# Routing numbers made between the output projection's slabs, and the sums of two norms with operands exchanged

## The reference

```python
x = first_block(...)            # ends: return rms_norm(h, norm_final)[:, N_META:]
mod = (c @ w_ada[l] + b_ada[l])[:, None, :]
shift1, scale1, gate1, shift2, scale2, gate2 = jnp.split(mod, 6, axis=-1)
h = rmsnorm(x, norm1_w[l]) * (1.0 + scale1) + shift1
proj = h @ w_in[l]
...
x = x + gate1 * (merged @ w_out[l])
h2 = rmsnorm(x, norm2_w[l]) * (1.0 + scale2) + shift2
x = x + gate2 * hierarchical_moe(h2, w_rg, b_rg, w_re, b_re, w_gate, w_up, w_down)

def hierarchical_moe(h, ...):
    g_logits = hf @ w_rg + b_rg                 # 4 groups
    pg = jax.nn.softmax(g_logits, axis=-1)
    pg_top, g_idx = lax.top_k(pg, 1)
    e_logits = hf @ w_re + b_re                 # 32 experts; those of the best group are looked at
    pe_top, j_idx = lax.top_k(softmax(e_sel), 2)
    weights = pg_top * pe_top / sum(pe_top)
    y = sum over the two experts of weight * (silu(hf @ w_gate[e]) * (hf @ w_up[e])) @ w_down[e]
```

## Time and profile before

| | |
|---|---|
| Median of 3 runs | 1809.47 us (1806.29 to 1811.33) |
| The profiled execution | 1804.85 us, its span 1803.0 us |
| PE busy | 1649.4 us, 91% of the span |
| DVE, ACT, POOL busy | 803.3, 541.7, 54.4 us |
| Mean granted clock of PE | 0.956 of full speed |
| HBM traffic | 268 MB, 149 GB/s over the span |

### The profile page before, as it was taken

The page is one execution under the profiler, slowest core; times in us unless marked ns, Lnnn a source line. Parts: engine busy times, 40 slices in busy tenths (PEclk is TensorE's granted clock), DMA queues, the critical chain, the costliest instruction groups (busy, mean ns, idle before and its releaser), DMA issues.

```text
span 1803.0 us, 20227 instructions
## 1 busy us (share of the span) xinstructions
PE 1649.4 (91%) x8343; PEld 1229.9 (68%) x8343; DVE 803.3 (45%) x1325; ACT 541.7 (30%) x851; POOL 54.4 (3%) x75
## 2 busy tenths in 40 slices
PE   3999999999997899999999999999999987987782
PEld 3996777777786688888888686797678855432330
DVE  5455334444452666665222864436653543110113
ACT  5234344354432322222112423322353312110111
POOL 3000000000000000000000000000000000111100
PEclk8999999999998899999998999999999987999997
DMA  4332212222232446473222222212123724999994
GB/s 130 106 94 70 71 48 71 71 71 71 67 98 94 140 157 219 162 233 130 104 94 65 70 71 71 70 48 71 48 71 140 264 113 162 417 419 421 419 381 161
DMA packets 146256, 260.33 MB, mean 144 GB/s; under 512 B 16036, under 2 KB 120640, under 8 KB 132464
## 3 DMA queue, kind: packets, MB, share of 16 engines
q1 hardware_dynamic: 140240, 249.82, 39.3%
q0 software_dynamic: 5920, 9.16, 1.4%
HBM read 253.71 MB, written 14.68 MB: 149 GB/s over the span
## 4 chain that ended last, share of the span: by engine, by line
PE 84%; DVE 7%; issue 4%; ACT 2%; DMA 2%; SPq 0%; POOLq 0%; DVEq 0%; ACTq 0%
PE psum L2220 20%; PE psum L2221 19%; PE psum L2222 19%; PE psum L2783 7%; PE psum L2800 3%; PE psum L2529 1%; PE psum L2518 1%; PE psum L2501 1%; PE psum L2761 1%; PE psum L2302 1%; DVE WL L1420 1%; PE psum L2410 1%; PE psum L2614 1%; PE psum L2713 1%; ACT Sb L1012 1%
## 5 line engine op out<-in xcount | busy, mean ns | idle before, releaser
L2220 PE MATMUL psum<-AH,WH 128*128 128x512 f32 (+1 forms) x1240 | 492.6, 397 | 16.5 <-DVE AL L1466 6.0
L2221 PE MATMUL psum<-AL,WH 128*128 128x512 f32 (+1 forms) x1240 | 476.3, 384 | 0.0
L2222 PE MATMUL psum<-AH,WL 128*128 128x512 f32 (+1 forms) x1240 | 473.0, 381 | 0.0
L1420 DVE TENSOR_TENSOR WL<-raw,WH 128x2048 fp32r<-128x2048 f32 (+1 forms) x100 | 226.6, 2267 | 207.8 <-ACT WH L916 207.3
L2220 PEld LDWEIGHTS psum<-AH,WH 128*128 128x128 f32 x1240 | 236.6, 191 | 81.5 <-issue 20.1
L2222 PEld LDWEIGHTS psum<-AH,WL 128*128 128x128 f32 x1240 | 237.0, 191 | 46.9
L2221 PEld LDWEIGHTS psum<-AL,WH 128*128 128x128 f32 x1240 | 237.0, 191 | 44.4 <-issue 3.1
L916 ACT ACTIVATE WH<-raw 128x2048 fp32r<-128x2048 f32 (+1 forms) x100 | 189.0, 1890 | 148.8 <-PE psum L2222 109.9
L2783 PE MATMUL psum<-WE,XT 128*64 128x512 f32 x544 | 131.0, 636 | 28.6 <-issue 27.7
L2783 PEld LDWEIGHTS psum<-WE,XT 128*64 128x64 f32 x544 | 47.4, 147 | 110.5 <-issue 110.5
L1833 DVE SCALAR_TENSOR_TENSOR cst<-araw,pcol,cst 128x256 f32<-128x256 f32 x168 | 81.6, 485 | 6.0
(11 more groups left out here) (483 smaller groups left out, 1891.4 us busy)
## 6 DMA issues: line engine op xcount, KB each, us to landing
raw<-w_in SPq DMA_DIRECT2D x45, 1024.0 KB, 5.2
WE<-w_gate SPq DMA_DIRECT2D x34, 1024.0 KB, 20.4
WE<-w_up SPq DMA_DIRECT2D x34, 1024.0 KB, 28.7
WE<-w_down SPq DMA_DIRECT2D x34, 1024.0 KB, 28.6
araw<-w_ada SPq DMA_DIRECT2D x24, 1024.0 KB, 6.4
raw<-w_ffn_in SPq DMA_DIRECT2D x22, 1024.0 KB, 5.3
raw<-w_ffn_out SPq DMA_DIRECT2D x11, 1024.0 KB, 4.9
raw<-w_out SPq DMA_DIRECT2D x8, 1024.0 KB, 5.1
```

The source lines that it names most:

```text
L1420: V.tensor_tensor(WL[:, n, 0:w], raw[:, n, 0:w], WH[:, fed[0] % HL, 0:w].bitcast(F32), ALU.subtract).then_inc(S_("lo_ready"), 1)
L2220: MM(dst, lh, rh, start=first, stop=False)
L2221: MM(dst, lh, rl, start=False, stop=False)
L2222: return MM(dst, ll, rh, start=False, stop=last)
```

## The change

1. **Norm sums between the blocks.** The squares of `hT` (now `nsq`, four buffers) are the moving operand, 512 tokens wide, and `wsq` the stationary one of two columns: one product for a chunk instead of four. The result is two rows of 512, which ACT copies and PE transposes back. ACT makes the first four squares ahead of `WH` of the next slab.
2. **Router beside the slabs of `wo2`.** The gain (1 + scale2) times norm2_w is multiplied into the router's weights, and shift2 times the weights into its bias, in slab `km` (`router_shift`, `router_scale`). The inverse root is one number for a token, so the logits can be taken from `hT` itself and scaled afterwards. `rows_of(c)` does, for each chunk, the sums of squares, the router's product and the transposes to token-major rows `xtm`; seven of the eight calls stand between pieces of the slabs.
3. **The rows stored for the experts** are now `xtm` times the inverse root only; gain and shift come in when the gathered rows are copied to `XT`, four operations of 128 columns in place of one of 512 on each of ACT and DVE. For that, gain and shift go through HBM once to change their layout (`gs_dram`).
4. **Routing.** `ranks` has 5 products instead of 14, the lists of tokens are made in bf16 (8 products as before, token ids split in two parts under 64), constants are made at the begin of `wo2`.
5. **Transfers.** The rows are stored by POOL instead of SP. Expert 1 is loaded one slab later, expert 17 after the last slab, expert 2 after the rows are stored, expert 18 right behind it.

```diff
@@ events
-                  ("dn", dict(squared=C1, summed=C1, bc=C1, **mean)), ("n_two", norm)]),
+                  ("dn", dict(squared=C1, summed=C1, bc=C1, **mean)), ("n_two", dict(squared=KC, summed=KC, **mean))]),
@@ SP
                 if s["name"] == ("wo2", 2):
                     sp.wait_ge(*when("m2_lo", KC))
                     load_expert(sp, 0, 1, NE // 2)
+                if s["name"] == ("wo2", 3):
                     load_expert(sp, 1, 0, 1)
-                if s["name"] == ("wo2", 3):
-                    load_expert(sp, 1, 1, NE // 2 + 1)
...
             sp.wait_ge(*when("dense_ready", len(GROUPS)))
+            load_expert(sp, 1, 1, NE // 2 + 1)
+            sp.wait_ge(*when("h2_stored", 16 * NB))
             load_expert(sp, 2, 0, 2)
-
-            for t in range(NB):
-                sp.wait_ge(*when("h2t_copied", 2 * t + 2))
-                sp.dma_start(h2_dram[P * t:P * t + P, :], h2t[:, t, :]).then_inc(S_("h2_stored"), 16)
-            sp.wait_ge(*when("spots_used", 1))
+            sp.wait_ge(*when("n_two_summed", KC))
+            load_expert(sp, 2, 1, NE // 2 + 2)
             sp.wait_ge(*when("overflow_ready", 1))
-            load_expert(sp, 2, 1, NE // 2 + 2)
@@ POOL
+            for t in range(NB):
+                pool.wait_ge(*when("h2t_copied", t + 1))
+                pool.dma_start(h2_dram[P * t:P * t + P, :], h2t[t]).then_inc(S_("h2_stored"), 16)
             pool.wait_ge(*when("h2_stored", 16 * NB))
             pool.wait_ge(*when("tokens_ready", 1))
             gather(0)
@@ ACT
+            def final_squares(n0, n1):
+                for n in range(n0, n1):
+                    freed(act, ("ffo", n))
+                    if n == 0:
+                        act.wait_ge(*when("mod_ready", 1))
+                    if n >= 4:
+                        act.wait_ge(*when("n_fin_summed", n - 3))
+                    nc.scalar.activation(nsq[:, n % 4, :], hT[:, n, :], ACT.Square).then_inc(S_("n_fin_squared"), 1)
...
+                if name == ("if", 0):
+                    final_squares(0, 4)
                 if split:
                     feed(s["h"] + 1)
...
-                    norm_squares("n_fin", hT, "ffo")
+                    final_squares(4, KC)
+                    act.wait_ge(*when("n_fin_summed", KC))
+                    nc.scalar.activation(nrst[0:2, :], bank(4)[0:2], ACT.Copy).then_inc(S_("n_fin_rows"), 1)
                     root("n_fin", stat[:, 44:48], stat[:, 40:44])
...
+            def rows_copy(c):
+                act.wait_ge(*when("x_major", c + 1))
+                nc.scalar.activation(xtm[:, :, P * c:P * c + P], bank(6 + c % 2).rearrange("p (t n) -> p t n", t=NB), ACT.Copy
+                                     ).then_inc(S_("xtm_copied"), 1)
...
+            def h2_copy(t):
+                nc.scalar.activation(h2t[t], xtm[:, t, :], ACT.Copy, scale=stat[:, 48 + t:49 + t]
                                      ).then_inc(S_("h2t_copied"), 1)
...
-                nc.scalar.activation(XT[:, t % 2, 0:512], bank(0), ACT.Copy).then_inc(S_("xt_even"), 1)
+                for k in range(4):
+                    nc.scalar.activation(XT[:, t % 2, P * k:P * k + P], bank(0, P, P * k), ACT.Identity, scale=gain8[:, k:k + 1],
+                                         bias=shift8[:, k:k + 1]).then_inc(S_("xt_even"), 1)
@@ DVE
+            def router_scale():
+                dve.wait_ge(*when("router_shift", 1))
+                link(V.tensor_tensor(rb, bank(6, NG + NE), rb, ALU.add))
+                dve.wait_ge(*when("router_landed", 32))
+                V.tensor_tensor(wr, wr, gain.unsqueeze(2).to_broadcast([P, KC, NG + NE]), ALU.mult).then_inc(S_("router_scaled"), 1)
...
-            norm_apply("n_two", hT, gain, False, out_name="h2_ready", shift=shift2, dst=H2)
...
-            dve.wait_ge(*when("logits_ready", 1))
+            dve.wait_ge(*when("n_two_summed", KC))
+            V.tensor_scalar(stat[:, 40:44], bank(4, 4), 1.0 / D, EPS, ALU.mult, ALU.add).then_inc(S_("n_two_ms"), 1)
+            dve.wait_ge(*when("n_two_root", 1))
+            V.reciprocal(stat[:, 48:52], stat[:, 44:48]).then_inc(S_("n_two_rms"), 1)
+            dve.wait_ge(*when("n_two_rms", 1))
+            dve.wait_ge(*when("router_mm", 1))
             link(V.tensor_tensor(lg, bank(5, NB * (NG + NE)).rearrange("p (t n) -> p t n", t=NB),
-                                 rb.unsqueeze(1).to_broadcast([P, NB, NG + NE]), ALU.add))
+                                 stat[:, 48:52].unsqueeze(2).to_broadcast([P, NB, NG + NE]), ALU.mult))
+            link(V.tensor_tensor(lg, lg, rb.unsqueeze(1).to_broadcast([P, NB, NG + NE]), ALU.add))
...
-            link(V.tensor_scalar(gaps, found, 0.5, NOBODY, ALU.is_lt, ALU.mult))
-            V.scalar_tensor_tensor(tok, found, -1.0, gaps, ALU.add, ALU.add).then_inc(S_("tokens_ready"), 1)
+            link(V.tensor_scalar(spot, found[:, 0, :], 32.0, None, ALU.mult))
+            link(V.tensor_tensor(spot, spot, found[:, 1, :], ALU.add))
+            link(V.tensor_scalar(gaps, spot, 0.5, NOBODY, ALU.is_lt, ALU.mult))
+            link(V.scalar_tensor_tensor(tok[:, 1, :], spot, -1.0, gaps, ALU.add, ALU.add))
+            V.tensor_scalar(tok[:, 0, :], tok[:, 1, :], 1, None, ALU.logical_shift_right).then_inc(S_("tokens_ready"), 1)
@@ PE
+            def rows_of(c):
+                pe.wait_ge(*when("n_two_squared", c + 1))
+                for t in range(NB):
+                    ins = MM(bank(4, 1, t), sq2[:, c % 4, P * t:P * t + P], ones[:, 0:1], start=c == t == 0, stop=c == KC - 1,
+                             skip_group_check=True)
+                ins.then_inc(S_("n_two_summed"), 1)
+                for t in range(NB):
+                    ins = MM(bank(5, NG + NE, (NG + NE) * t), hT[:, c, P * t:P * t + P], wr[:, c, :], start=c == t == 0,
+                             stop=c == KC - 1, skip_group_check=True)
+                if c == KC - 1:
+                    ins.then_inc(S_("router_mm"), 1)
+                if c >= 2:
+                    pe.wait_ge(*when("xtm_copied", c - 1))
+                for t in range(NB):
+                    ins = nc.tensor.transpose(bank(6 + c % 2, P, P * t), hT[:, c, P * t:P * t + P], ident)
+                ins.then_inc(S_("x_major"), 1)
...
                     for n in range(KC):
                         pe.wait_ge(*when("n_fin_squared", n + 1))
-                        for t in range(NB):
-                            ins = MM(bank(4, 2, 2 * t), ntmp[:, n % 2, P * t:P * t + P], wsq[:, n, :], start=n == t == 0,
-                                     stop=n == KC - 1, skip_group_check=True)
-                        ins.then_inc(S_("n_fin_summed"), 1)
+                        MM(bank(4)[0:2], wsq[:, n, :], nsq[:, n % 4, :], start=n == 0, stop=n == KC - 1
+                           ).then_inc(S_("n_fin_summed"), 1)
+                    pe.wait_ge(*when("n_fin_rows", 1))
+                    for t in range(NB):
+                        ins = nc.tensor.transpose(bank(4, 2, 2 * t), nrst[0:2, P * t:P * t + P], ident[0:2, 0:2])
+                    ins.then_inc(S_("n_fin_turned"), 1)
...
+                        if s["name"][0] == "wo2":
+                            i = s["name"][1]
+                            if (i, j) == (1, 0):
+                                rows_of(0)
+                            if i and j == 1:
+                                rows_of(2 * i - 1)
+                            if i and j == 2:
+                                rows_of(2 * i)
                     end(s)
-            norm_pe("n_two")
...
+            rows_of(KC - 1)
```

More of the change, by code:

```diff
@@ L1188, in begin @@
                     split_merged("m2", merged2, ("gate2", 1, 1, 1), 4 if k == "wo2" else 0)
+                if name == ("wo2", 0):
+                    nc.scalar.activation(small[:, 244:245], eps, ACT.Sqrt).then_inc(S_("act_chain"), 1)
+                    chain.n += 1
+                if name == ("if", 0):
+                    final_squares(0, 4)
                 if split:
@@ L1289, in end @@
                         nc.scalar.activation(sq, hT[:, c, :], ACT.Square).then_inc(S_(tag + "_squared"), 1)
+                        if k == "wo2" and c >= 2:
+                            rows_copy(c - 2)
                 if k in ("qm", "km"):
@@ L1881, in begin @@
                                                ).then_inc(S_("m2_lo"), 1)
+                if name == ("wo2", 0):
+                    routing_numbers()
                 if split:
@@ L2534, in ranks @@
                 pe.wait_ge(*when("choices", 1))
[L2535 to L2539 removed]
+                pe.wait_ge(*when("xtm_copied", KC))
+                MM(bank(7, NB * NE), K("strict"), both.rearrange("p t n -> p (t n)"), start=True, stop=False, skip_group_check=True)
+                for b in range(1, NB + 1):
+                    n = NE * (NB + 1 - b)
+                    ins = MM(bank(7, n, NE * b), ones, both.rearrange("p t n -> p (t n)")[:, 0:n], start=False, stop=b == NB,
+                             skip_group_check=True)
```

(10 more changed lines are left out.)

225 lines of the change are left out of this document (100 added, 125 removed).

## The result

The changed kernel takes 1790.20 us (median of 6 runs, 1789.09 to 1795.15), the kernel before 1805.11 (6 runs, 1803.10 to 1811.33): ratio 0.9919, 95% interval 0.9907 to 0.9930, so 14.6 us less (12.6 to 16.8). Forecast were 8.7 us less and 1800.8, in a range of 1795 to 1807. The two profiled executions have spans of 1803.0 and 1787.3 us, 15.7 apart. Of these, 1.7 is no effect of the change: the slabs up to the first touched place are the same code, and are done 1.74 us earlier.

The account below looks back on a forecast made before the run. The prediction took the expert stage's weight stream, and the chain ahead of its start, as the bound. Its terms, 1.4 - 12.7 + 15.0 + 3.9 + 2.4 - 0.6 - 0.7 = 8.7 us, gave 1809.5 - 8.7 = 1800.8 us, range 1795 to 1807.

Parts of the forecast that it names:

- Part 1: Norm sums between the blocks: earlier squares and exchanged operands let DVE go on 1.4 us earlier, bounds -1 to 5.3.
- I take the fall at the same 979: Sums between the blocks: PE's clock falls to half at 979 as before, so the sums end at 983.5, middle 984.8.
- The rival with full clock: Sums between the blocks: the turned sums keep full clock, done at 981.2, gain 5 us, time 1797; chance 0.14.
- Part 2: Slab `km`: ten small products and three DVE operations hide under PE's wait, cost 0, without that cover 2 us.
- Part 3: PE between output slab pieces: seven chunks of 2.3 us make the slabs end 12.7 us later, bounds 11.5 to 15.
- Rival one: Output slabs: the clock falls behind each burst; all seven falls cost 14 us, 1815; chance 0.07, and 0.12 for one to four.
- Part 4: Slabs' end to logits: logits ready 4.15 us behind the end instead of 19.2, a gain of 15.0 us.
- Part 5: Routing chain after logits: counting gains 3.9 us, token lists 2.4; indices cost 0.6, pair 0's `XT` 0.7; gather 0.
- Part 6: Expert stage: each pair takes 0.7 us longer, 13.5 instead of 12.8, costing nothing under the stream's 14.7.
- distance: Expert stage: 235 us from the first load of expert 3 to the last gate and up; growth would show the forecast wrong.
- passed on whole: Expert stage: the earlier start moves the end equally; the rival, not passed on, gave 1805 if half is lost, chance 0.08.

Follow-up runs that it names:

- e1: The kernel before with only four squares ahead of the weights' copy, sums' operands exchanged and two rows turned back: 1798.16 us, ratio 0.9961 to the kernel before.
- e2: The changed kernel with squares still ahead but the sums in the old form, 64 products of two streamed columns: 1793.89 us, ratio 0.9942 to the kernel before.
- e13: The changed kernel with each exchanged sums product of 512 columns cut into four of 128: 1791.70 us, ratio 0.9921 to the kernel before.
- e4: The changed kernel with DVE's five token operations ahead of its five on overflow experts: 1790.06 us, ratio 0.9926 to the kernel before.
- e3: The changed kernel with all eight chunks' sums, router products and row transposes behind the last output slab: 1800.35 us, ratio 0.9976 to the kernel before.
- e5: The changed kernel with expert 18's load held until the rows of pair 0 have landed: 1784.70 us, ratio 0.9892 to the kernel before.
- e11: The changed kernel with three more ACT operations of 64 columns ahead of ACT's half of each XT copy: 1797.35 us, ratio 0.9965 to the kernel before.
- e8: The changed kernel with six more ACT operations of 64 columns ahead of ACT's half of each XT copy: 1822.91 us, ratio 1.0094 to the kernel before.
- e7: The changed kernel with expert 18 held until pair 0's rows land and token operations ahead of the overflow ones: 1784.21 us, ratio 0.9887 to the kernel before.
- e14: The changed kernel with expert 18 held, token operations first, 6 unread TensorE products behind counting and 5 behind the token lists: 1781.01 us, ratio 0.9863 to the kernel before.
- e6: The changed kernel with expert 2 issued without waiting for the row stores, so experts 17, 2, 18 follow each other: 1789.34 us, ratio 0.9915 to the kernel before.

## Why the prediction was wrong in size

**The base, 4.4 of the 10.6 us missed.** The profiled execution of the kernel before took 1804.85 us. I added 4.6 to reach the median of three runs, 1809.47. Six runs have their median at 1805.11: the profile was close to the typical run and all three were longer. Had I kept to the profile, 1796.2, the forecast would have missed by 6.0, and the range moved down by 4.6 would have begun at 1790.4, within 0.2 of the result.

**Part 1, +1.4 expected, 5.6 measured: the step that failed.** It is the sentence "I take the fall at the same 979", by which the sums would end at 984.8, 10.5 us behind their start; they took 7.04. It rested on rows 10 and 11, three products followed by a half clock, and on none that showed such products in a longer stretch. The clock stayed full (e1), for the form's sake (e2), and with many loads as well (e13). The rival with full clock had the mechanism, with a chance of 0.14; between bounds of -1 and 5.3 I had chosen below the middle. Of the 5.6, the earlier start is 1.7, the sums 4.5 and the spreading, now in part at full clock, 1.0; copy and turning took 1.1 back (1.4 counted), and of ACT's table load of 1.28 us, which I hadn't seen, DVE's root waits for some 0.6. In the kernel before the load lay under the sums, at 985.03.

**Part 2, 0 expected, 0.** The changed kernel's profile has no fall of the clock at 1040 to 1050 and the others do, e4 and e13 with the same code there too, so 0.65 us of its lead is chance.

**Part 3, -12.7 expected, -11.8.** A chunk is 2.18 us (2.3); the clock never fell, transposes or not. Rival one didn't come, and e3 shows that its mechanism exists, at 5.7 us.

**Part 4, +15.0 expected, +14.9.** Logits at +4.25 for +4.15.

**Part 5.** Counting +3.8 (3.9). From the last indicator to the gather +1.4 for 1.8: the lists gained 3.1 for 2.4, but became so short (0.6 us) that DVE's overflow operations ended after them, a new wait of 1.1 us. The gather -0.5 for 0; that it starts behind expert 18's loads was right, its length was left open between 4.3 and 11.1, and e5 shows that it was a choice of order. Row transposes -0.7 for 0, since PE stood idle ahead of them and ran at half clock; `XT` -0.9 for -0.7; gate and up +0.4 for 0.

**Part 6, 0 expected.** Pairs of 13.69 for 13.5, distance 235.0 for 235.6 before: passed on whole, and 0.6 more.

Together 5.6 - 11.8 + 14.9 + 3.8 + 1.4 - 0.5 - 1.6 + 0.4 + 0.6 = 12.8, and 0.3 each from small DVE operations and behind the last gate and up: 13.4. With the 1.7 and 0.65 that are chance these are the 15.7 us between the spans, to a tenth. The runs say 14.6 (12.6 to 16.8).

## What to carry to other kernels

Where a reduction on TensorE can be written with its long side streamed instead of loaded, count it at full clock, and bound it by both clocks; the gain here was not in fewer instructions but in the clock. Narrow work was cheap in pieces of 2.2 us between full products, and nearly twice as dear from the sixth microsecond of one long stretch on. When a change takes PE's side work out from beside a transfer, look at the transfer's order next: it was worth 1.4 us before and 5.5 after. And take the base of a forecast from as many runs as there are: here its error, 4.4 us, was as large as the failed step's, 4.2.

## What the runs showed of the hardware

- The clock fell 2 to 2.5 us into products with two columns streamed against 128 columns of weights (before and e2), and stayed through 7 us of 512 or 128 columns streamed against two columns of weights (the changed kernel and e1; e13).
- It stayed at 1.00 through seven stretches of 2.18 us of narrow products and transposes between full ones, and fell 5.7 us into one long stretch of them (e3).
- Where PE and not the stream was the bound, waits of 2.62 and 3.52 us ahead of each down product went with a fall in every second pair and in every pair (e11, e8). Where PE also waited for the stream, falls were rare: one in the changed kernel, with a wait of 3.40 us that brought none, three in e5, four in the kernel before.
- The first gather, 0.5 MB, took 3.8 to 4.1 us with no load of weights ahead of it (e5, e7, e14), 7.9 to 9.1 behind 3 MB and more (e3, e1). GpSimd's stores of 0.5 MB took 5.1 to 6.3 us in the changed kernel, and 8.6 to 15.4 beside 9 MB (e6).
- ACT's table load ahead of the root took 1.28 us; it counted only where nothing else was waited for.
- The executions of one kernel on one chip spread over 2 to 12 us (e14, e1 without its longest); the profile alone doesn't tell where in this it lies.
